# One fused, unrolled attention stage in an RWKV-7 and grouped-query attention encoder layer

## What is computed

```python
q = _rmsnorm(q.reshape(B, T, ATT_Q_HEADS, ATT_HEAD), q_norm)      # 8 query heads of 128
k = _rmsnorm(k.reshape(B, T, ATT_KV_HEADS, ATT_HEAD), k_norm)     # 2 key heads
v = v.reshape(B, T, ATT_KV_HEADS, ATT_HEAD)
q = _apply_rope(q, cos, sin)      # x * cos + rot(x) * sin; rot swaps blocks of 32 rows, one of them negated
k = _apply_rope(k, cos, sin)
s = jnp.einsum('bqhgd,bkhd->bhgqk', qi, k).astype(jnp.float32) * scale
p = jax.nn.softmax(s, axis=-1).astype(v.dtype)
o = jnp.einsum('bhgqk,bkhd->bqhgd', p, v)
```

## Time and profile before

| | us |
|---|---|
| median of 3 runs | 3773.07 (3767.62 to 3775.22) |
| the profiled execution: its own time | 3774.45 |
| the profiled execution: span from first to last instruction | 3772.7 |
| of this, until the heads stage begins its loads | 20.4 |
| heads stage, from there to the first scores | 20.4 to 341.3 |
| core stage, to the first loads of the next stage | 341.3 to 759.3 |
| the rest, which the change leaves as it is | 759.3 to 3772.7 |

### The profile page before, as it was taken

How to read it: one execution, slowest core, us unless ns; L and a number is a source line. 1 busy time by engine, 2 the same in 40 slices (tenths; PEclk the granted TensorE clock), 3 DMA queues, 4 the chain that set the end, 5 groups by cost and what they waited for, 6 DMA issues and landing times. The chain is left out here.

```text
span 3772.7 us, 60069 instructions
## 1 busy us (share of the span) xinstructions
PE 3418.5 (91%) x25508; PEld 2242.8 (59%) x25508; DVE 1831.9 (49%) x3142; ACT 997.0 (26%) x1554; POOL 55.2 (1%) x103
## 2 busy tenths in 40 slices
PE   6888888679999959988999979999899999999998
PEld 3446666435554535546888875455666666666665
DVE  1223555416786766832554542313655545564546
ACT  1212333203433421332333335500132111121111
POOL 0100000000000000000000000000000000000000
PEclk9999999889999979999999989999999999999999
DMA  2000000113353441324443432211112212212221
GB/s 108 22 11 0 0 0 0 42 58 110 126 170 117 143 173 68 118 92 167 125 134 123 126 117 106 85 63 69 56 56 67 75 60 67 67 61 102 67 67 62
DMA packets 195705, 309.75 MB, mean 82 GB/s; under 512 B 49552, under 2 KB 155024, under 8 KB 190352
## 3 DMA queue, kind: packets, MB, share of 16 engines
q1 hardware_dynamic: 195472, 306.31, 24.0%
HBM read 211.26 MB, written 95.03 MB: 81 GB/s over the span
## 5 line engine op out<-in xcount | busy, mean ns | idle before, releaser
L597 PE MATMUL ra_ps<-xT,ra_w 128*128 128x512 f32 (+1 forms) x1152 | 432.0, 528 | 19.9 <-DMA ra_w<-in_w_in 17.4
L597 PEld LDWEIGHTS ra_ps<-xT,ra_w 128*128 128x128 f32 x1152 | 215.0, 190 | 220.6 <-issue 193.2
L1624 PE MATMUL tl_ps<-merged,tl_sums 128*128 128x320 f32 x1088 | 322.4, 436 | 15.4 <-DVE oR L1817 7.9
L965 PE MATMUL rg_ps<-xT,rg_w 128*128 128x512 f32 (+1 forms) x768 | 285.4, 528 | 18.0 <-DMA rg_w<-in_w_gate 18.0
L1624 PE MATMUL tl_ps<-merged,tl_wt 128*128 128x320 f32 x896 | 271.5, 438 | 9.1 <-DMA tl_wt<-in_w_out 9.1
L1817 DVE TENSOR_TENSOR oR<-tl_ps,oR 128x320 f32<-128x320 f32 x416 | 202.2, 490 | 151.4 <-PE tl_ps L1624 149.2
L1624 PEld LDWEIGHTS tl_ps<-merged,tl_sums 128*128 128x128 f32 x1088 | 206.3, 191 | 109.7 <-issue 28.2
L1624 PE MATMUL tl_ps<-tl_Th,tl_sums 128*128 128x320 f32 x864 | 242.9, 438 | 8.4 <-issue 6.1
L965 PEld LDWEIGHTS rg_ps<-xT,rg_w 128*128 128x128 f32 x768 | 144.8, 192 | 138.1 <-issue 114.0
L1624 PEld LDWEIGHTS tl_ps<-merged,tl_wt 128*128 128x128 f32 x896 | 172.7, 193 | 82.3 <-DMA tl_wt<-in_w_out 9.5
L52 PE MATMUL qk_ps<-xT,qk_w 128*128 128x512 f32 (+1 forms) x480 | 184.3, 547 | 38.1 <-DMA qk_w<-in_w_in 24.1
(11 more groups left out here) (244 smaller groups left out, 4879.7 us busy)
## 6 DMA issues: line engine op xcount, KB each, us to landing
rc_ub<-ub SPq DMA_DIRECT2D x80, 640.0 KB, 5.3
ub<-ra_ub SPq DMA_DIRECT2D x32, 1280.0 KB, 5.4
tl_wt<-in_w_ff SPq DMA_DIRECT2D x32, 1024.0 KB, 4.8
tl_wt<-in_w_ff SPq DMA_DIRECT2D x64, 512.0 KB, 3.5
ra_w<-in_w_in SPq DMA_DIRECT2D x24, 512.0 KB, 3.5
ub<-ra_v SPq DMA_DIRECT2D x16, 640.0 KB, 6.2
gates<-rg_gate SPq DMA_DIRECT2D x16, 640.0 KB, 3.9
mg_gate<-gates SPq DMA_DIRECT2D x16, 640.0 KB, 3.9
```

Source lines behind the costliest of these rows:

```text
L597: last = pe.matmul(ps[:, bank + j, 0:n], w[c][:, 128 * i:128 * i + 128], xT[:, i, t0:t0 + n], start=(i == 0), stop=(i == KT - 1))
L965: last = pe.matmul(ps[:, 3 * (b % 2) + j, 0:n], w[b % 3][:, 128 * i:128 * i + 128], xT[:, i, t0:t0 + n], start=(i == 0), stop=(i == KT - 1))
L1624: last = pe.matmul(bank(n, b), lhs(k), rhs(k), start=(fresh and k == 0), stop=(k == d - 1), skip_group_check=True)
```

## The change

Load, heads and core become one stage, `attention_stage` (tag `at`), without a loop or a register. What it does:

- The first weights and x come in nine transfers, and the first head's products go block by block of x as it lands; the other loads follow behind.
- One head at a time, key heads first. PE goes on to the next head's projection at once, and the three sums of squares of a head (`stat`) are put between the spans of the next one, in PSUM banks of their own. For the last head they stand between the first groups of v.
- The product with `perm` goes. SP copies the blocks of 32 partitions crosswise from `zq` to `zr`, in four transfers a head, and the sign is in the sine table. POOL does nothing; both multiplications and the sum are DVE's.
- Queries and keys stay in one tile `qk`, and PE reads queries there (no `qt`).
- Tiles are in groups: four tiles of one head (two for the short sequence). The product with v is made for a whole group in 512 (256) columns, and spread over the tiles of the group behind it.
- DVE's order for a tile is: copy of the transposed row, reciprocal and normalisation of the next tile, maximum of the tile after that, and once a group the output.
- Each group's output goes to DRAM on its own.

Cut to its core (`GROUPS`, `TILES` and `FIRST` list groups, tiles and each group's first tile; `values_after(t)` is the share of the last group's key blocks that stands behind tile t):

```diff
+            def load(i):
+                sp.dma_start(w[:, i % 3, :], hbm["w_in"][B_Q + HEADS[i]]).then_inc(w_ready[i % 3], 16)
+            load(0)
+            for k in range(KT):
+                sp.dma_start(xT[:, k, :], hbm["xT"][128 * k:128 * k + 128, :]).then_inc(x_ready[k], 16)
+            load(1)
+            sp.dma_start(cst[:, :], hbm["consts"]).then_inc(c_ready, 16)
+            sp.dma_start(glob[:, 0:NGLOB], hbm["glob"]).then_inc(c_ready, 16)
+            sp.dma_start(cos[:, :], hbm["cos"]).then_inc(tab_ready, 16)
+            sp.dma_start(sin[:, :], hbm["sin"]).then_inc(tab_ready, 16)
+            load(2)
...
+            for i in range(NH):
+                if i + 3 < NH:
+                    sp.wait_ge(z_ready, i + 1)
...
+                sp.wait_ge(zn_done, i + 1)
+                after(sp, head_done, i)
+                for a, b in ((0, 32), (32, 0), (64, 96), (96, 64)):
+                    sp.dma_start(zr[a:a + 32, :], zq[i % 2][b:b + 32, :]).then_inc(zr_ready, 16)
+            for g in range(len(GROUPS)):
+                h, t0, _, _, n = GROUPS[g]
+                sp.wait_ge(o_done, g + 1)
+                sp.dma_start(hbm["o_att"][:, h, t0:t0 + 128 * n], ot[g % 2][:, 0:128 * n]).then_inc(o_sent[g % 2], 16)
...
+                for j, (t0, n) in enumerate(SPANS):
+                    for k in range(KT):
+                        last = pe.matmul(ps[:, z_bank(i) + j, 0:n], w[:, i % 3, 128 * k:128 * k + 128], xT[:, k, t0:t0 + n],
+                                         start=(k == 0), stop=(k == KT - 1))
+                    if j == 2:
+                        last.then_inc(z_ready, 1)
+                    stat(i - 1, j)
...
+            def transposes(t):
+                pe.wait_ge(p_done, t + 1)
+                after(pe, t_dve, t)
+                after(pe, t_act, t)
+                n = halves(t)
+                for k in range(2 * n):
+                    last = pe.transpose(ps[:, 4 + k // n, 128 * (k % n):128 * (k % n) + 128], p[t % 2][:, 128 * k:128 * k + 128], ident)
+                last.then_inc(t_ready, 1)
...
+            def values(g, ks):
+                h, _, k0, nk, _ = GROUPS[g]
+                kv, n = h // (QH // KVH), columns(g)
+                end = FIRST[g] + GROUPS[g][4]
...
+                    last = pe.matmul(ps[:, 6 + g % 2, 0:n], vt[:, k0 // 128 + k, HD * kv:HD * kv + HD], pT[g % 2][:, k, 0:n],
+                                     start=(k == 0), stop=(k == nk // 128 - 1))
+                    if k == nk // 128 - 1:
+                        last.then_inc(o_ready, 1)
...
+            for i in range(NH):
+                head(i)
+            for t in range(T // 128):
+                if t == 0:
+                    for j in range(2):
+                        pe.wait_ge(w_ready[(NH + j) % 3], 16 * ((NH + j) // 3) + 16)
+                value_rows(t)
+                if t < 3:
+                    stat(NH - 1, t)
+            pe.wait_ge(v_done, T // 128)
+            pe.wait_ge(head_done, NH)
+            scores(0)
+            scores(1)
+            for t in range(NT):
+                transposes(t)
+                if t + 2 < NT:
+                    scores(t + 2)
+                if TILES[t][0]:
+                    values(TILES[t][0] - 1, values_after(t))
+            values(len(GROUPS) - 1, range(GROUPS[-1][3] // 128))
...
+            def roots(i):
+                for j, (t0, n) in enumerate(SPANS):
+                    act.wait_ge(stat_ready, 3 * i + j + 1)
+                    if i and j == 0:
+                        act.wait_ge(zn_done, i)
+                    act.activation(rt[:, t0:t0 + n], ps[:, 6 + (3 * i + j) % 2, 0:n], ACT.Ln, bias=cst[:, C_EPS:C_EPS + 1],
+                                   scale=D / HD).then_inc(ln_done, 1)
+                act.wait_ge(ln_done, 3 * i + 3)
+                act.activation(rt[:, :], rt[:, :], ACT.Exp, scale=-0.5).then_inc(rt_done, 1)
+            act.wait_ge(c_ready, 32)
+            for i in range(NH):
+                act.wait_ge(z_ready, i + 1)
+                after(act, stat_ready, 3 * i)
+                act.activation(sq[:, :], set_of(ps, z_bank(i)), ACT.Square).then_inc(sq_done, 1)
+                if i < NH - 1:
+                    roots(i)
+            for t in range(T // 128):
+                act.wait_ge(v_ready, t + 1)
+                act.activation(vt[:, t, :], ps[:, t % 3, 0:KVH * HD], ACT.Copy).then_inc(v_done, 1)
+                if t == 2:
+                    roots(NH - 1)
+            def exponents(t):
+                c, n = t % 2, keys_of(t)
+                act.wait_ge(nm_done, t + 1)
+                if t >= 2:
+                    act.wait_ge(t_ready, t - 1)
+                    act.wait_ge(ri_done, t - 1)
+                act.activation(p[c][:, 0:n], scores_of(t), ACT.Exp, bias=nm[:, c:c + 1], scale=ATT_SCALE,
+                               accum_out=rs[:, c:c + 1]).then_inc(exp_done, 1)
+            def transposed(t):
+                g, i = TILES[t]
+                n = halves(t)
+                act.wait_ge(t_ready, t + 1)
+                if g >= 2 and i == 0:
+                    act.wait_ge(o_ready, g - 1)
+                act.activation(pT[g % 2][:, n:2 * n, 128 * i:128 * i + 128],
+                               ps[:, 5, 0:128 * n].rearrange("p (k q) -> p k q", q=128), ACT.Copy).then_inc(t_act, 1)
+            exponents(0)
+            exponents(1)
+            for t in range(NT):
+                transposed(t)
+                if t + 2 < NT:
+                    exponents(t + 2)
...
+            def head_sum(i):
+                x = qk[:, HEADS[i], :]
+                dve.wait_ge(zr_ready, 64 * i + 64)
+                dve.tensor_tensor(zr[:, :], zr[:, :], sin[:, :], ALU.mult).then_inc(sin_done, 1)
+                dve.wait_ge(sin_done, i + 1)
+                dve.wait_ge(cos_done, i + 1)
+                dve.tensor_tensor(x, x, zr[:, :], ALU.add).then_inc(head_done, 1)
...
-                    wide(pe, ps, 3 * s, ones, sq[s]).then_inc(stat_ready, 1)
-                for s in range(2):
-                    pe.wait_ge(zn_ready, i * 2 + s + 1)
-                    wide(pe, ps, 3 * s, perm, zq[s]).then_inc(rot_ready, 1)
...
-                    for c in range(2):
-                        transposes(run, i * 2 + (base + c), c)
-                        scores(run, i * 2 + (base + c + 2), c)
-                        values(run, i * 2 + (base + c), c)
-                for c in range(2):
...
-                with dve.Fori(0, tiles // 2 - 1, 1) as i:
-                    for c in range(2):
-                        transposed(run, i * 2 + (base + c), c)
-                        probabilities(run, i * 2 + (base + c + 1), 1 - c)
-                        output(run, i * 2 + c, i * 2 + (base + c), c)
...
+            maxima(0)
+            maxima(1)
+            normalise(0)
+            for t in range(NT):
+                g, i = TILES[t]
+                transposed(t)
+                if t + 1 < NT:
+                    normalise(t + 1)
+                if t + 2 < NT:
+                    maxima(t + 2)
+                if g and i == GROUPS[g][4] - 1:
+                    output(g - 1)
+            output(len(GROUPS) - 1)
...
-            attention_core(nc, hbm, cst, qs, qp, ks, kp, vt)
+        attention_stage(nc, hbm, xT, cst, glob)
...
-    return np.cos(ang), np.sin(ang)
+    turn = np.where((np.arange(HD) // 32) % 2 == 0, -1.0, 1.0).astype(np.float32)
+    return np.cos(ang), np.sin(ang) * turn[:, None]
```

387 lines of the change are left out of this document (152 added, 235 removed).

## The result

The changed kernel takes 3565.4 us (median of 4 runs, 3562.72 to 3566.13) against 3770.35 for the kernel before on the same chip: a ratio of 0.9457, 95% interval 0.944 to 0.9473. The forecast was 3581 with 3567 to 3612 as its range. The profiled execution has a span of 3564.3 us and a time of its own of 3566.13.

What follows compares the result with a forecast made beforehand. PE, busy 91% of the span, was taken to bound the kernel. The heads part gives 100 us and the core 92, together 191.6, from 3774.45 to 3582.9 profiled, 3581 as median; range 3567 to 3612, held at 0.80.

Steps and rivals of the forecast that it cites:

- full tiles: Core, 60 tiles of 1,024 keys with values beside them: PE's own work sets the pace, 4.36 us each.
- short tiles: Core, 256-key tiles: two with values at 4.1 us, 14 at 2.1 us, ruled by the DVE and ACT chain.
- the end: End of the attention stage: last values, copy, a 128 KB transfer and the barrier take 6.3 us.
- the code behind the mark: Everything after the next stage's first load (the mark): same code on the same tiles, taken as unchanged.
- stops in v: Product of v: PE waits about 1.0 us for the squares and about 2.5 us for an Ln.
- Per head 17.19 plus the three sums: Heads: projection 17.19 us plus sums of squares 2.15 make 19.34 a head, 174.1 for nine.
- ACT's chain: Heads: last sum, Ln, table load, Exp, next square end 4.9 us after the projection; PE asks at 7.3.
- the copies' 5 us: Rotation in the heads: the swap transfers take 5 us a head, and up to 14.8 is free.
- The widening alone saves only 0.23 a tile, the new order 0.8: Core: wider values products save 0.23 us a tile, DVE's new order 0.8.
- loads show: Rival in the core: four weight loads of 0.19 us add 0.76 a tile, 49 us, giving 3630; chance 0.03.
- the core keeps its pace: Rival: a closed chain of maximum and scores keeps tiles at 5.42 us, losing 64 us, giving 3646; chance 0.05.
- slow copies: Rival in the rotation: head period is 4.5 us plus copy; chance 0.02 below break-even (34 us a head), 0.02 above.

Runs made afterwards that it cites:

- experiment 6: Changed kernel with each head's swap in 32 transfers of 4 partitions instead of 4 of 32: 3634.21 us, ratio 0.9639.
- experiments 1 and 2: Changed kernel with DVE's maximum before the next tile's normalisation again: 3629.75 us; changed kernel with the values product in 128 columns again: 3557.53 us.
- experiment 7: Changed kernel without the maximum in the 16 short tiles, a constant instead: short tiles 1.28 us apart instead of 1.70.
- Experiments 9 and 10: Changed kernel with 64, 128, 256 semaphore increments heading PE's list: 3551.46, 3585.18, 3600.86 us; 64 heading ACT's list: 3565.91; 64 at PE's scaled-stage start: 3558.05.
- 64 and with 128 increments: Changed kernel with that many semaphore increments ahead of PE's first product: 3551.46 and 3585.18 us.

## Why the prediction was wrong, point by point

Its mechanisms held in the attention stage; three terms (full tiles, short tiles, the end) were sized too large, a fourth, the code behind the mark, was put at no change without a reason that holds, and one loss was not foreseen. The terms of its sum, in the order of the prediction; "off" is measured less forecast:

| term | forecast | measured | off |
|---|---|---|---|
| first head ends | 25.9 | 25.4 | |
| a head | 19.34 | 19.34 | |
| stops in v | 1.0 and 2.5 | 0.9 and 2.5 | |
| first scores and fill, to | 247.4 | 248.3 | +0.9 |
| four tiles without values | 14.8 | 15.1 | +0.3 |
| 60 full tiles | 261.6 | 256.0 | -5.6 |
| two short tiles with values | 8.2 | 8.2 | 0 |
| 14 short tiles | 29.4 | 23.8 | -5.6 |
| the end | 6.3 | 3.5 | -2.8 |
| behind the mark | 3013.4 | 3009.4 | -4.0 |

That is 16.8 us, the whole distance of the profiled execution (3566.13) from the 3582.9 worked out for it. Luck is in it too: the forecast took the full clock throughout, and the stretch from v to the fifth tile ran at 0.95, which cost some 3.2 us (60.9 us at 1.00). With the full clock the time would have been that much further below the range.

- *"Per head 17.19 plus the three sums"*: right. So were the order of the stops, ACT's chain and the copies' 5 us, though a forecast of one copy's price is not what the heads depend on: experiment 6 shows that they feel it only beyond 14.8.
- *"60 x 4.36"*: the mechanism right, two sizes off, 5.6 us together, for which the range had nothing below. The 58 true ones take 4.31 (2.9 us in sum). The last two have short scores beside them and take 3.03 (2.7 us); that could have been read off the code, where tile t carries the scores of t + 2.
- *"The widening alone saves only 0.23 a tile, the new order 0.8"*: the order is worth 0.88, the widening 0.07 (experiments 1 and 2). The 0.23 was worked out from the duration of a row in which 16 records overlap by a tail, where the prediction elsewhere goes by starts. For the sum it made no difference.
- *"The chain of DVE and ACT rules: I take 2.1"*: this is the step that failed first, a term mis-sized. The chain rules (experiment 7), but at 1.70, and the bound of 1.83 given to it from below was no bound. It was put together of 740.77 - 739.34 and a whole duration, 0.35, which makes 1.78; where its last 0.05 comes from the prediction doesn't say. But the next instruction of DVE starts 0.27 after the start of a normalisation of 0.35, which makes 1.43 + 0.27 = 1.70, the measured figure. On top of this I added 0.3 for the copy and the output; they fall into the gaps of the chain and cost nothing. Together 5.6 us, where the range gave the term 4 to move.
- *"A transfer of 128 KB (3.0) and the barrier (1.0)"*: the changed kernel's page of the profile has 1.7 us from issue to landing for these transfers, and last values, copy, landing and barrier go more into each other than their sum. 2.8 us, for which the range had no term of its own.
- *"All that comes later is the same code on the same tiles, and I take it as the same"*: wrong by 4 us in these two traces, and a second trace of the kernel before has 3019.5 there instead of 3013.4. What holds in both traces of each kernel is the state stage, 511.4 and 511.8 before, 505.8 and 503.5 now. It is the same code in another place: PE's list ahead of it has another number of instructions, its first product moves from record 249 to 231 of a block of 256, and PE's gaps in it are 17.5 and 17.9 us in sum before, 14.2 and 11.6 now. Experiments 9 and 10 show that such a shift alone moves these stages: over the shifts tried, between 569.1 and 585.2 in the scaled one, 494.1 and 504.1 in the state stage. That a shift of 18 records makes the 5.6 us is argued from this and was not tried; six of the kernels here have the list at the same place, and their state stages still differ from 499.6 to 506.1. The range was built without this, and so was the statement that a changed time after the mark would show an error in the change.
- *The rivals*: "loads show" is refuted by four wide records in 1.72 us with their loads beside them; "the core keeps its pace" is what happens with the old order (5.19), but not with the new; "slow copies" has the right formula and the wrong case.

The full tiles (5.6), the small tiles (5.6) and the code behind the mark (4.0) make up most of the miss; without any one of the three the time would have been inside the range, by 2 to 4 us. The attention stage itself is 3.6 us shorter from PE's first product to the mark with 64 and with 128 increments (545.3 and 545.3, against 548.9 and 549.1 with none and 256). Of this 3.2 is the granted clock from v to the fifth tile, 1.00 in the first two and 0.95 in the other two; the remaining 0.4 lies in the heads. That x has landed when PE begins does not explain it, since it holds for 256 as well, and why the clock stays up in some kernels is open.

## What to carry to other kernels

Read a chain's period off starts alone, also its last link: a duration holds a tail that the next instruction doesn't wait for, and in a loop of 1.7 us such a tail was 5% of it. When a closed chain is the pace, look for the two links whose order in one engine's list closes it; to exchange them was worth 64 us here, the wider product 4. Look at the granted clock before a few us are put down to an edit: two kernels with the same work and the same waits took 64.1 and 60.9 us for one stretch. And when an edit changes the number of PE's instructions, unchanged code behind it can move by some 20 us in 3,000: compare stage by stage before an effect under 1% is put down to the edit, and try a few shifts in a place where PE is idle ahead of a barrier.
